# Hybrid attention block and differential-attention/convolution block, one core: nine modulation parts by transposes, the first modulation in halves on another queue, the bias table behind a panel

## The reference

```python
# first block
mod = jax.nn.silu(c) @ w_ada + b_ada                  # w_ada (1024, 3072)
shift, scale, gate = jnp.split(mod, 3, axis=-1)
h = rms_norm(x, norm_gain) * (1 + scale) + shift
proj = h @ w_in                                       # 13 parts: q, k, v, z, kc, vc, ...
o_a = banded_gqa(...)                                 # window 128, bias by distance, sinks
o_b = g0 * o_cmp + g1 * o_sel + g2 * o_win            # compressed, selected, window 512
out = concat(o_a * silu(z_a), o_b * silu(z_b)) @ w_out
x = x + gate * out
# second block: two layers, i = 0 (differential attention), i = 1 (short convolution)
mod   = silu(c)     @ ada_w[i] + ada_b[i]             # ada_w (1024, 6144): sh1, sc1, g1, sh2, sc2, g2
mod_c = silu(c_ctx) @ ada_w[i] + ada_b[i]             # for the context, only shift and scale are used
h = h + g1 * mixer(rmsnorm(h, norm1[i]) * (1 + sc1) + sh1)
h = h + g2 * swiglu(rmsnorm(h, norm2[i]) * (1 + sc2) + sh2)
```

## Time and profile before

| | |
|---|---|
| median of 3 executions | 1791.21 us |
| lowest, highest | 1784.34, 1792.2 us |
| the profiled execution | 1788.7 us |
| its span, first to last instruction | 1786.9 us |
| TensorE matmul busy | 1720.8 us (96%) |
| VectorE busy | 976.8 us (55%) |
| ScalarE busy | 679.1 us (38%) |
| GpSimd busy | 61.2 us (3%) |
| mean granted TensorE clock | 0.972 |

### The profile page before, as it was taken

One profiled execution on the slowest core, in us unless ns is written; L12 is line 12 of the kernel. 1 busy time (PEld: TensorE's weight loads), 2 busy tenths in 40 slices (PEclk: granted clock), 3 DMA queues, 4 the chain that ended last, 5 costly groups with the idle time before them and its releaser, 6 DMA issues.

```text
span 1786.9 us, 23061 instructions
## 1 busy us (share of the span) xinstructions
PE 1720.8 (96%) x8968; PEld 1411.6 (79%) x8968; DVE 976.8 (55%) x1803; ACT 679.1 (38%) x1417; POOL 61.2 (3%) x119
## 2 busy tenths in 40 slices
PE   4899999999999999899999999999999899999999
PEld 2777777777999999777788887887888788888887
DVE  4666466666866776666555554346555533333232
ACT  3434555554545555554222222223222422222221
POOL 0000000000000000000000000000000000000000
PEclk8899997899999999998999999998999999999999
DMA  8886332212223131221666555432443233333332
GB/s 302 218 244 162 97 92 86 71 37 72 65 60 99 45 99 44 83 61 38 188 187 184 174 175 156 121 109 84 120 125 97 71 95 94 95 94 95 97 110 77
DMA packets 290215, 202.02 MB, mean 113 GB/s; under 512 B 76247, under 2 KB 272072, under 8 KB 289082
## 3 DMA queue, kind: packets, MB, share of 16 engines
q1 hardware_dynamic: 266942, 133.21, 26.5%
q0 software_dynamic: 15536, 56.37, 10.5%
q10 hardware_dynamic: 7628, 10.97, 1.8%
HBM read 197.33 MB, written 5.28 MB: 113 GB/s over the span
## 4 chain that ended last, share of the span: by engine, by line
PE 88%; DVE 6%; ACT 2%; issue 2%; DMA 2%; ACTq 1%; SPq 0%; DVEq 0%
PE PS L858 13%; PE PS L859 13%; PE PS L860 13%; PE PS L841 5%; PE PS L842 4%; PE PS L840 4%; PE PS L1283 3%; PE PS L1285 3%; PE PS L1284 3%; PE PS L1088 3%; PE PS L1333 2%; PE PS L1357 2%; PE PS L1062 2%; PE PS L1070 1%; PE PS L1345 1%
## 5 line engine op out<-in xcount | busy, mean ns | idle before, releaser
L2014 DVE TENSOR_TENSOR WL<-WS,WH 128x512 fp32r<-128x512 f32 x416 | 268.3, 687 | 269.7 <-ACT WH L1506 269.2
L1506 ACT ACTIVATE WH<-WS 128x512 fp32r<-128x512 f32 x416 | 237.7, 621 | 182.5 <-PE PS L842 140.4
L858 PE MATMUL PS<-A3H,WL 128*128 128x512 f32 x672 | 267.3, 398 | 0.0
L859 PE MATMUL PS<-A3L,WH 128*128 128x512 f32 x672 | 266.5, 397 | 0.0
L860 PE MATMUL PS<-A3H,WH 128*128 128x512 f32 x672 | 264.2, 393 | 0.0
L858 PEld LDWEIGHTS PS<-A3H,WL 128*128 128x128 f32 x672 | 126.2, 188 | 33.5 <-issue 2.8
L860 PEld LDWEIGHTS PS<-A3H,WH 128*128 128x128 f32 x672 | 126.2, 188 | 31.0
L859 PEld LDWEIGHTS PS<-A3L,WH 128*128 128x128 f32 x672 | 126.2, 188 | 28.9
L841 PE MATMUL PS<-GL,WH 128*128 128x512 f32 x352 | 139.7, 397 | 0.0
L840 PE MATMUL PS<-GH,WL 128*128 128x512 f32 x352 | 139.0, 395 | 0.4 <-DVE WL L2014 0.4
L842 PE MATMUL PS<-GH,WH 128*128 128x512 f32 x352 | 139.3, 396 | 0.0
(11 more groups left out here) (362 smaller groups left out, 3506.8 us busy)
## 6 DMA issues: line engine op xcount, KB each, us to landing
AW<-in_ada_w POOLq DMA_DIRECT2D x96, 512.0 KB, 4.2
WS<-in_ffn_w_gate_up SPq DMA_DIRECT2D x88, 512.0 KB, 4.2
WS<-in_ffn_w_down SPq DMA_DIRECT2D x32, 512.0 KB, 4.1
WS<-in_sc_w_in SPq DMA_DIRECT2D x24, 512.0 KB, 3.9
AB<-in_w_ada SPq DMA_DIRECT2D x8, 1024.0 KB, 16.0
WS<-in_w_in SPq DMA_DIRECT2D x32, 256.0 KB, 4.3
WS<-in_diff_w_qkv SPq DMA_DIRECT2D x64, 128.0 KB, 2.6
WS<-in_ffn_w_down SPq DMA_DIRECT2D x16, 384.0 KB, 3.4
```

What stands on the lines that cost most here:

```text
L858: mm(PS[:, b, :], wl[:, k, :], hi[:, k, 0:S], start=(k == 0), stop=False)
L859: mm(PS[:, b, :], wh[:, k, :], lo[:, k, 0:S], start=False, stop=False)
L1506: f(weights(p)[0][:, k, :], WS[:, p % 2, k, :], ACT.Copy).then_inc(w_hi, 1)
L2014: tt(lo[:, k, :], WS[:, p % 2, k, :], hi[:, k, :].bitcast(F32), ALU.subtract).then_inc(w_lo, 1)
```

## The change

Three edits, all outside the large products.

1. *Nine parts by transposes.* e0, e1, g0, g1, h0 and the four parts of up0 are no longer summed over partitions by TensorE. TensorE turns the 8 tiles of sums (a transpose against the identity, 128 columns each), and VectorE adds up along the row with tensor_reduce into FOLD and adds the bias. In attention a part takes two small jobs of four tiles (e0 and e0b, ...), one PSUM bank each, so there are 47 small jobs; e0 moves from step 1 to step 0. In up0 the 8 tiles go to banks 5 and 6 at once.
2. *First modulation by halves of the features.* The weights AB are sent as sixteen loads of 0.5 MB, in pieces of 2 KB, by GpSimd, once all small rows have landed. SyncE sends the kcvc panels in their place. VectorE adds up the first 512 features of shift and scale over all 8 row tiles, then the other 512; TensorE sums each half into its own bank; VectorE normalizes tiles 0 to 3 with the first half and 4 to 7 with the second. Two copies of bias rows and the rounding of the kcvc panels change their place (ScalarE does the copies; the panels are rounded before the root; VectorE's small gains come after the normalization).
3. *The bias table.* ScalarE still writes the 16 rows; the two copies are issued by SyncE between the loads of z0 and z1.

```diff
@@ -49,13 +49,13 @@
-    ("ada_a", 1, 0, 0, 1, 0),
+    ("ada_a", 1, 0, 0, 0, 0),
...
     ("gate", 1, 1, 1, 0, 0),
-    ("att", 1, 12, 0, 42, 6),
+    ("att", 1, 12, 0, 47, 6),
     ("w_out2", 1, 4, 0, 0, 0),
...
-SMALL_AT.update({"e0": 1, "e1": 2, "y0": 11, "y1": 19, "l0": 22, "t00": 25, "y2": 27, "t01": 29, "w0": 33, "y3": 35, "g0": 37, "g1": 41, "c0": 54, "c1": 63, "c2": 66, "c3": 86})
+SMALL_AT.update({"e0": 0, "e0b": 1, "e1": 2, "e1b": 3, "y0": 11, "y1": 19, "l0": 22, "t00": 25, "y2": 27, "t01": 29, "w0": 33, "y3": 35, "g0": 37, "g0b": 38, "g1": 41, "g1b": 42, "c0": 54, "c1": 63, "c2": 66, "c3": 86})
-SMALL_AT.update({"h0": 70, "lam": 74, "y7": N_ATT})
+SMALL_AT.update({"h0": 70, "h0b": 71, "lam": 74, "y7": N_ATT})
 ATT_SMALLS = sorted(SMALL_AT, key=lambda name: SMALL_AT[name])
...
@@ -613,6 +615,10 @@
             c = slice(f * P, (f + 1) * P)
             eng.dma_start(out[0].rearrange("(t p) d -> p t d", p=P)[:, :, c], OUT[:, :, c]).then_inc(done, 16)
 
+        def block_of_ada(x, b):
+
+            return x.rearrange("p (h n) -> p h n", h=2)[:, :, D // 2 * b:D // 2 * (b + 1)]
+
         def small_rows():
 
             def rows_of(a):
@@ -658,10 +664,6 @@
-            w_ada = ins["w_ada"][0].rearrange("(k p) n -> k p n", p=P)
-            for k in range(KT):
-                sp.dma_start(AB[:, k, :], w_ada[k, :, 0:2 * D]).then_inc(ada_loaded[k], 16)
-
             def panel(a, j, src, kts=8, cols=P):
...
@@ -696,6 +698,12 @@
             a = At("z")
             for j in range(8):
                 head_pair(a, j, (ZB if j >= 4 else ZA) * P + j % 4 * HD)
+                if j == 0:
+                    sp.wait_ge(rows_out, 16)
+                    for head, at, n in ((0, 3 * P - 1, 2 * P), (8, P - 1, S)):
+                        sp.dma_start(dist_table[head:head + 8, :, 0:n],
+                                     bass.AP(dist_rows.tensor, head * 640 + at, [[640, 8], [-1, P], [1, n]]))\
+                            .then_inc(dist_out, 16)
                 if j >= 5:
                     hidden_in(j - 5)
             a = At("gate")
@@ -782,9 +790,15 @@
         def _(pool):
             pool.memset(VEC[:, :, :], 0.0).then_inc(vec_zero, 1)
             pool.memset(EPSC[:, :], EPS).then_inc(eps_set, 1)
+            w_ada = ins["w_ada"][0].rearrange("(k p) n -> k p n", p=P)
+            pool.wait_ge(vec_in, 16 * len(small_rows()))
+            for b in range(2):
+                for k in range(KT):
+                    pool.dma_start(block_of_ada(AB[:, k, :], b), block_of_ada(w_ada[k, :, 0:2 * D], b))\
+                        .then_inc(ada_loaded[4 * b + k // 2], 16)
 
             pool.wait_ge(cs_ready, 1)
-            pool.wait_ge(small_free, At("ada_a").small(0) + 1)
+            pool.wait_ge(ada_added, 2)
             pool.wait_ge(rows_out, 16)
             pool.memset(VCP[:, :, :], 0.0).then_inc(cz_zero, 1)
             pool.memset(KCN[:, :, :], 0.0).then_inc(cz_zero, 1)
@@ -894,9 +908,22 @@
                 pe.wait_ge(part_sum, sums_before(n + 1))
                 add_up(a, u, AA[:, n % 2, :])
 
-            def add_context(a, u, n):
+            def turn_sums(name, n, sums, half):
+
                 pe.wait_ge(part_sum, sums_before(n + 1))
-                add_up(a, u, AC[:, :])
+                bank = take_small(att, att_small(name))
+                for f in range(4):
+                    c = (4 * half + f) * P
+                    m = tp(bank[:, f * P:(f + 1) * P], sums[:, c:c + P], IDENT)
+                m.then_inc(small_done, 1)
+
+            def turn_layer_part(a, u, n):
+
+                pe.wait_ge(part_sum, sums_before(n + 1))
+                take_small(a, u)
+                for f in range(KT):
+                    m = tp(FLAT[:, FOLD_BANK * S + f * P:FOLD_BANK * S + (f + 1) * P], AA[:, n % 2, f * P:(f + 1) * P], IDENT)
+                m.then_inc(small_done, 1)
 
             def add_beside(a, u, n, bank):
 
@@ -944,14 +971,13 @@
                 if f:
                     add_square(f - 1)
             add_square(KT - 1)
-            a = At("ada_a")
-            take_small(a, 0)
-            for half in range(2):
-                pe.wait_ge(ada_used, 2 * KT - 2 + half)
-                for f in range(KT):
-                    m = mm(PS[:, SMALL, KT * half + f:KT * half + f + 1], AA[:, half, f * P:(f + 1) * P], ONES[:, 0:1],
-                           start=True, stop=True)
-            m.then_inc(small_done, 1)
+            for b in range(2):
+                pe.wait_ge(ada_used, KT * (b + 1))
+                for half in range(2):
+                    for f in range(4 * b, 4 * b + 4):
+                        m = mm(PS[:, 6 - b, KT * half + f:KT * half + f + 1], AA[:, half, f * P:(f + 1) * P], ONES[:, 0:1],
+                               start=True, stop=True)
+                m.then_inc(ada_summed, 1)
 
             a = At("kcvc")
             linear_pair(a, A1H, A1L, 0)
...
@@ -1445,7 +1464,7 @@
                     if l == 0 and a.i in TAKES:
-                        add_part(At("ada6"), TAKES.index(a.i), 6 + TAKES.index(a.i))
+                        turn_layer_part(At("ada6"), TAKES.index(a.i), 6 + TAKES.index(a.i))
                 for a, _ in passes(pe, f"down{l}"):
                     for t in range(2):
                         b = take_acc(a, t)
@@ -1565,6 +1584,9 @@
             a = At("mods1")
             act.wait_ge(small_free, a.small(0) + 1)
             f(CS[:, :], VT[:, V_C:V_C + 24], ACT.Silu).then_inc(cs_ready, 1)
+            for k in range(2):
+                act.wait_ge(small_done, a.small(2 + k) + 1)
+                f(US[:, k * 320:(k + 1) * 320], PS[0:16, SMALL, 0:320], ACT.Copy).then_inc(small_free, 1)
 
             a = At("x_in")
             act.wait_ge(eps_set, 1)
@@ -1579,13 +1601,10 @@
             act.wait_ge(small_free, a.small(3) + 1)
             act.dma_start(dist_rows, US[:, :]).then_inc(rows_out, 16)
 
-            act.wait_ge(rows_out, 16)
-            for head, at, n in ((0, 3 * P - 1, 2 * P), (8, P - 1, S)):
-                act.dma_start(dist_table[head:head + 8, :, 0:n],
-                              bass.AP(dist_rows.tensor, head * 640 + at, [[640, 8], [-1, P], [1, n]]))\
-                    .then_inc(dist_out, 16)
+            for j in range(2):
+                split(At("kcvc"), j)
             load_set(LN_AND_EXP)
-            layer_norm("norm_a", 0, A1H, slice(0, S), M1, first_panels=At("kcvc"))
+            layer_norm("norm_a", 0, A1H, slice(0, S), M1)
 
             def split_hidden(q):
 
@@ -2059,20 +2078,31 @@
                 tt(cut(dst, at, 4), bank[:, 0:4], cut(VT, v, 4), ALU.add).then_inc(read, 1)
                 tt(cut(dst, at + 4, 4), bank[:, 4:8], cut(VT, v + 4, 4), ALU.add).then_inc(small_free, 1)
 
-            def add_ada():
-
-                both = AA[:, :, :].rearrange("p a n -> p (a n)")
+            def add_ada(b):
+
+                sums = AA[:, :, D // 2 * b:D // 2 * (b + 1)]
                 for k in range(KT):
-                    dve.wait_ge(ada_loaded[k], 16)
+                    if k % 2 == 0:
+                        dve.wait_ge(ada_loaded[4 * b + k // 2], 32)
+                    src = block_of_ada(AB[:, k, :], b)
                     if k == 0:
-                        m = ts(both, AB[:, k, :], CS[:, k:k + 1], None, ALU.mult)
-                        m.then_inc(ada_used, 1)
+                        ts(sums, src, CS[:, k:k + 1], None, ALU.mult).then_inc(ada_used, 1)
                     else:
-                        dve.wait_ge(ada_used, 2 * k - 1)
-                        for half in range(2):
-                            c = slice(D * half, D * (half + 1))
-                            stt(both[:, c], AB[:, k, c], CS[:, k:k + 1], both[:, c], ALU.mult, ALU.add)\
-                                .then_inc(ada_used, 1)
+                        dve.wait_ge(ada_used, KT * b + k)
+                        stt(sums, src, CS[:, k:k + 1], sums, ALU.mult, ALU.add).then_inc(ada_used, 1)
+
+            def take_ada(b):
+
+                dve.wait_ge(ada_summed, b + 1)
+                tt(view(M1[:, 4 * b:], [8, 2], [1, 4]), view(PS[:, 6 - b, 4 * b:], [8, 2], [1, 4]),
+                   view(VT[:, V_BADA + 4 * b:], [8, 2], [1, 4]), ALU.add).then_inc(ada_added, 1)
+                dve.wait_ge(ada_added, b + 1)
+                stt(NS[:, 4 * b:4 * b + 4], M1[:, 8 + 4 * b:12 + 4 * b], 1.0, VT[:, V_NG + 4 * b:V_NG + 4 * b + 4],
+                    ALU.add, ALU.mult).then_inc(ada_added if b else ln_scale, 1)
+                if b:
+                    dve.wait_ge(ada_added, 3)
+                else:
+                    dve.wait_ge(ln_scale, 1)
 
             def layer_norm(L, R, src, hi, lo, tok, scale, shift, gain, rs, n=S, tiles=range(KT)):
 
@@ -2113,24 +2143,22 @@
-                dve.wait_ge(small_done, a.small(2 + k) + 1)
-                copy(US[:, k * 320:(k + 1) * 320], PS[0:16, SMALL, 0:320]).then_inc(small_free, 1)
-
+            dve.wait_ge(cs_ready, 1)
+            add_ada(0)
+            add_ada(1)
```

(37 more changed lines are left out.)

39 lines of the change are left out of this document (14 added, 25 removed).

## The result

| | before | changed |
|---|---|---|
| median of 20 executions | 1785.82 us | 1791.94 us |
| lowest, highest | 1777.51, 1793.86 us | 1785.48, 1797.34 us |
| the profiled execution | 1788.7 us | 1791.97 us |
| its span | 1786.9 us | 1790.1 us |
| mean granted TensorE clock | 0.972 | 0.973 |

The ratio is 1.0029, 95% interval 1.0018 to 1.0041: the changed kernel is slower by 5.2 us, a small difference, but one that 20 executions of each tell from none. The forecast was 1784.5 us, some 5 us faster. The range of 1772 to 1795 holds 1791.94, but the direction was wrong.

The account below looks back on a forecast made before the run. TensorE was taken to bound the kernel (busy 1720.8 of 1786.9 us), except at the start. Terms 3.1 - 7.7 + 0.9 + 1.5 - 3 = -5.2 us gave 1783.5 or 1786.0, placed at 1784.5 us, range 1772 to 1795.

Parts of the forecast that it names:

- The sums of the first modulation: At the start: last load lands at 38.2, sums ready at 40.9 (39.5 to 43 open); alone this part gains 5.2 us.
- the two 0.5 MB panels that SyncE now sends first add about 1 us: At the start: the kcvc panels overlapping the modulation loads move the last landing from 37.2 to 38.2.
- Rival B: First modulation: GpSimd's sixteen 2 KB-piece loads come slower, the last 9 us later; 1793.5 us in all; chance 0.13.
- z1 behind the table: On SyncE's queue z1's panel lands after the table, at 67.5 against 64.39; hidden_part(0) moves by +3.1 us.
- Rival A: z1 is not held by the table: +3.1 becomes -5.2, in all -13.5, 1776 us; chance 0.22.
- "What is freed, ScalarE's queue from 35.60 on, brings nothing more": At the start: freeing ScalarE's queue of the table gains nothing, as the root waits for nothing and the adds end later.
- Nine parts, 7.7 us: Attention and up0: eight transposes take 0.88 us where a part cost 1.74 on TensorE; nine parts give -7.7 us.
- VectorE's idle 3.16 us: In up0: VectorE idles before its product against a reduce of at most 1.4 us, so four parts give their full gain.
- the folds: In attention: VectorE's folds of ten half-parts, partly exposed to TensorE, cost +1.5 us (0 to 6.5).
- e0's wait: In attention: e0 at step 0 waits for ScalarE's log to free its bank, about +0.9 us.
- The clock: In attention: half of the one-column blocks go, so less time at the lower clock; -3 us (-8 to +4).
- The sum: Whole kernel: 3.1 - 7.7 + 0.9 + 1.5 - 3 = -5.2 us, forecast 1784.5 us.

Follow-up runs that it names:

- panels_later: The changed kernel with SyncE's two kcvc panels held until the first pair of modulation weights landed, and its three W2 loads until the last; ratio 1.0005.
- rows_later: The changed kernel with SyncE's three small W2 loads held until the last modulation weights have landed; ratio 1.0022.
- ada_sync: The changed kernel with the sixteen loads of the first modulation on SyncE's queue ahead of the kcvc panels, in place of GpSimd's; ratio 0.9989.
- table_pool: The changed kernel with the two bias table copies issued by GpSimd behind its sixteen loads, in place of SyncE between z0 and z1; ratio 0.9994.
- up0_table_halves: The kernel before with up0's parts by transposes folded one step later, table copies by GpSimd, and modulation by halves with its sixteen loads on SyncE; ratio 1.0013.
- table_sync_alone: The kernel before with only the two bias table copies moved from ScalarE to SyncE, between z0 and z1; ratio 0.9997.
- up0_late_alone: The kernel before with only up0's four parts by transposes, their fold one step later, behind the next panel's low-part split; ratio 0.9953.
- up0_and_table: The kernel before with up0's four parts by transposes, folded one step later, and the table copies issued by GpSimd; ratio 0.9937, median 1776.2 us.
- parts_alone: The kernel before with only the nine parts by transposes, e0 at step 0; first modulation and bias table as before; ratio 0.9985.
- throttled: The changed kernel with GpSimd sending its sixteen loads two pairs at a time, each once the pair before the last has landed; ratio 1.0048.
- whole_loads: The changed kernel with the modulation weights as eight 1 MB loads in 8 KB pieces on GpSimd's queue; ratio 1.0078 from two executions.

## Why the prediction was wrong

*The sums of the first modulation* (forecast 40.9, measured 48.8) are the step that failed, and in it the landing of the first pair of loads, which the forecast never worked out by itself. The forecast took the last landing plus one pair of adds. That rule held: the last load was issued at 24.09 and landed 21.7 us later, at 45.8 (DMA view), and the adds ended at 48.8. Wrong was the landing itself, forecast at 38.2. From the first pair on, the rate was as forecast too: the eight pairs landed over 17.9 us, 2.5 us apart, where seven eighths of the forecast's 21.2 us are 18.6. VectorE needs 2.6 us for the adds of a pair and so could not make up what was lost. All of the loss lies ahead of the first pair. By the forecast's own numbers (bytes from 16.0, an eighth of 21.2, 1 us for the panels) it lands near 19.7; it landed at 28.0.

The term that was mis-sized is "the two 0.5 MB panels that SyncE now sends first add about 1 us". Holding them back brought the first add 4.9 to 5.5 us forward (panels_later against rows_later and against the changed kernel), and 4.3 against the earliest of the runs that have them ahead. From 12 to 20 us the DMA engines moved 184 GB/s in the changed kernel, 0.49 MB of it weights and 0.93 MB SyncE's; in before they moved 277 GB/s in the same window (DMA view). Of the 9.1 us to the 18.92 of ada_sync 3.6 remain. They are about as long as GpSimd's wait for the small rows (first issue 12.56 in place of 8.52), and behind the issue the pair's second load takes about as long on both queues, 9.0 us in panels_later and 9.8 in ada_sync; no run takes that wait away alone. Rival B named the right place, a late GpSimd queue, and nearly the right time (1793.5), for a wrong reason: once it ran, the rate was near before's (380 GB/s from 20 to 33 us, against 417). It had the last landing 9 us late and measured are 7.6, but from another cause, so that its time came so close is luck.

*z1 behind the table* was right as a mechanism and nearly in size: the split is released by its load, 22.7 us after z0 was sent where the forecast had 25.3, and taking the table off SyncE's queue gives 6.9 us at the split and 5.5 at hidden_part(0). It stood at 72.78 and not 67.5 because z0 was sent at 50.1 and not 42.2, which is the first failure again. With either of the two alone taken away, hidden_part(0) stands at 91.2 (ada_sync) or 92.1 (table_pool), still behind before's 89.59. Rival A did not come true; table_pool shows a difference of 5.5 us by the issuing engine alone, so it matters what a load stands behind. In up0_table_halves the copies from another queue still made two panels 9 and 12 us late. By the Trainium skill's section "Issuing engines are not separate DMA queues" (DMA: Bandwidth & Descriptors), as rival A read it, table_pool would have shown no difference but that of the issue time; that all transfers share the same engines, which it also states, agrees with up0_table_halves.

*"What is freed, ScalarE's queue from 35.60 on, brings nothing more"* held in the changed kernel, for the reason given: ScalarE's log is done by 35 us, and TensorE's two groups of sums (38.66 and 48.90) both wait for VectorE's adds. It doesn't hold for the edit by itself. Where the adds end at 40.2, the sums stand behind the log at 41.09, which stands behind the table's issue at 35.60, and moving the issue away brought the first product forward by 2.7 us (table_sync_alone).

*Nine parts, 7.7 us.* In up0 the size was right: a block of eight transposes stands 0.79 us ahead of the next product against 1.70 for the column sums, 4 x 0.91 = 3.6 us, and 3.9 us in up0_late_alone. But VectorE's idle 3.16 us do not lie between the fold and the next panel's split: they end before the fold starts, and from the fold to that split VectorE is busy without a gap. The fold pushes the split, and TensorE waits 0.5 us four times. In attention the folds cost 4.8 us on TensorE and not 1.5 (within the bound of 6.5; at g0, where the earlier trace rows showed no slack, 2.3 in one place), e0's wait was 1.0 (forecast 0.9), and the five parts came out at nothing or a small loss.

*The clock*, -3 us: the sign came true in the changed kernel (0.94), but the runs don't show it as an effect of the transposes.

| attention, us at granted clock | |
|---|---|
| column sums (before, up0_late_alone, table_sync_alone, up0_and_table, up0_table_halves) | 248.4 at 0.92, 248.5 at 0.91, 245.5 at 0.93, 245.1 at 0.93, 245.2 at 0.93 |
| transposes (changed, parts_alone, rows_later, table_pool, ada_sync, throttled, panels_later, whole_loads) | 245.6 at 0.94, 248.4 at 0.92, 251.2 at 0.91, 248.9 at 0.92, 246.0 at 0.94, 245.7 at 0.94, 248.5 at 0.92, 248.4 at 0.92 |

The means are 246.5 and 247.8. At equal clock the transposes are never shorter: 251.2 against 248.5 at 0.91, and 248.4 to 248.9 against 248.4 at 0.92. A term of 3 us with a sign had no ground; plus or minus 3 had. By the Trainium skill (TensorE: Matmul & The Clock Gate, Part 4) a transpose does not count as TensorE being busy in the same way, and the term would have been 0 or above. These means neither show nor refute that rule; as a guess of the term it was the better one.

*The sum*, for the profiled pair: start +7.95 (forecast +3.1), attention -2.8 (forecast -4.3 + 0.9 + 1.5 - 3 = -4.9), up0 +0.3 (forecast -3.4; 2.2 us went into the waits for WL, and the stretch at its start ran at a lower clock, 13.8 us in place of 12.3), the other stages -2.3 (forecast 0). Together +3.2 against -5.2. The 1784.5 itself rested in part on a median of three executions, 1791.21; over 20 executions that kernel's median is 1785.82, so a forecast of -5.2 from there would have been 1780.6, further off.

## What to carry to other kernels

When a step follows a series of loads, work out the landing of the first load as well as the last. Here loads and adds kept the same pace (2.5 and 2.6 us a pair), so a first pair that was 8 us late stayed 8 us late to the end. In that sum, what other queues send just ahead belongs to the first landing: here 1 MB of panels was worth some 5 us and not 1. A transfer that nobody waits for soon goes neither ahead of a panel in its queue nor ahead of ScalarE's next load of a function table: give it a queue that has nothing else to do, and a time when no needed panel is under way. An engine's idle time helps only if it lies between the added work and the work that others wait for; a fold of 1.2 us cost 0.5 us four times at one place of the step and nothing at another.
